# Narrow experts with two groups of 64 columns, large and small experts in turns, and weight slots of 512 columns

## The reference, cut to what matters

```
logits = xf @ router_w + router_b            # 1024 tokens x 32 experts
top_val, top_idx = top_k(logits, 4); gates = softmax(top_val)
for each expert e, with the rows xb of the tokens that chose it:
    gate, up = split(xb @ w_gu[e] + b_gu[e]) # w_gu[e]: 1024 x 2048
    gate = min(gate, 7); up = clip(up, -7, 7)
    y = ((up + 1) * gate * sigmoid(1.702 * gate)) @ w_down[e] + b_down[e]
    h[token] += gate_of_token * y            # w_down[e]: 1024 x 1024
```

## Time and profile before

| | us |
|---|---|
| median of 3 runs | 2329.13 |
| the profiled execution | 2327.12 |
| its span, first to last instruction | 2325.5 |
| TensorE busy (matmul) in it | 2261.4 |
| VectorE, ScalarE, GpSimd busy | 751.5, 374.1, 587.9 |

### The profile page before, as it was taken

The page is one execution under the profiler, slowest core; times in us unless marked ns, Lnnn a source line. Parts: engine busy times, 40 slices in busy tenths (PEclk is TensorE's granted clock), DMA queues, the critical chain, the costliest instruction groups (busy, mean ns, idle before and its releaser), DMA issues.

```text
span 2325.5 us, 36694 instructions
## 1 busy us (share of the span) xinstructions
PE 2261.4 (97%) x14520; PEld 1898.0 (82%) x14521; DVE 751.5 (32%) x1759; ACT 374.1 (16%) x845; POOL 587.9 (25%) x808
## 2 busy tenths in 40 slices
PE   8999998999987999999999999999999999999997
PEld 5664447768757999999999999998878878878876
DVE  2134776545541162222222222222222222222224
ACT  2222553323320001001111111110000000000002
POOL 1132222232232122222222222322222222222222
PEclk9999999999998999999999999999999999999999
DMA  7000213011119666777788888899999999999996
GB/s 260 1 1 19 29 35 142 28 46 37 56 37 305 220 215 217 227 228 244 254 262 270 278 270 283 283 296 317 332 323 338 321 326 337 324 328 336 324 327 229
DMA packets 377669, 506.07 MB, mean 218 GB/s; under 512 B 14887, under 2 KB 290795, under 8 KB 377448
## 3 DMA queue, kind: packets, MB, share of 16 engines
q1 hardware_dynamic: 362632, 459.56, 59.3%
q0 software_dynamic: 14864, 44.14, 7.2%
HBM read 472.17 MB, written 34.14 MB: 218 GB/s over the span
## 4 chain that ended last, share of the span: by engine, by line
PE 69%; DMA 0%; DVE 0%; issue 0%; POOL 0%; POOLq 0%; DVEq 0%
PE ps L1757 44%; PE ps L1784 12%; PE ps L1769 10%; PE ps L1736 2%; PE ps L1745 1%; DMA arena<-h_dram,arena 0%; DVE arena L1902 0%; DVE arena L2009 0%; POOL out L1636 0%; DVE arena L2015 0%; DVE arena L1995 0%; POOL small L226 0%; DVE small L223 0%; DVEq L2012 0%; POOLq L1636 0%
## 5 line engine op out<-in xcount | busy, mean ns | idle before, releaser
L1757 PEld LDWEIGHTS ps<-arena 128*128 128x128 f32 x8192 | 1029.6, 190 | 8.8 <-issue 7.7
L1757 PE MATMUL ps<-arena 128*128 128x128 f32 (+15 forms) x8192 | 1035.8, 288 | 0.8 <-DVE arena L1902 0.8
L1926 DVE TENSOR_SCALAR arena<-ps,arena 128x128 f32<-128x128 f32 (+15 forms) x256 | 94.6, 370 | 1109.9 <-PE ps L1757 1109.1
L1596 POOL TENSOR_TENSOR arena<-arena 128x128 f32<-128x128 f32 (+15 forms) x256 | 132.0, 516 | 878.0 <-DVEq L1933 878.0
L1668 ACT ACTIVATE arena<-arena 128x128 f32<-128x128 f32 (+15 forms) x256 | 83.3, 325 | 1212.5 <-DVE arena L1926 1212.5
L1784 PE MATMUL ps<-arena 128*128 128x224 f32 (+14 forms) x1920 | 272.4, 303 | 0.0
L1784 PEld LDWEIGHTS ps<-arena 128*128 128x128 f32 x1920 | 270.1, 189 | 0.2
L1769 PE MATMUL ps<-arena 128*128 128x512 f32 x544 | 236.3, 592 | 0.0
L1769 PEld LDWEIGHTS ps<-arena 128*128 128x128 f32 x544 | 102.0, 190 | 122.0 <-issue 121.7
L530 PE MATMUL ps<-arena 128*128 128x384 f32 (+1 forms) x512 | 171.7, 494 | 2.1 <-DVE arena L633 2.1
L530 PEld LDWEIGHTS ps<-arena 128*128 128x128 f32 x512 | 97.5, 193 | 68.3 <-issue 2.7
(11 more groups left out here) (274 smaller groups left out, 1617.2 us busy)
## 6 DMA issues: line engine op xcount, KB each, us to landing
arena<-in_exp_w_gu SPq DMA_DIRECT2D x256, 1024.0 KB, 7.7
arena<-in_exp_w_down SPq DMA_DIRECT2D x64, 2048.0 KB, 9.2
arena<-in_exp_b_down SPq DMA_DIRECT2D x17, 512.0 KB, 10.8
arena<-in_x SPq DMA_DIRECT2D x16, 512.0 KB, 9.0
arena<-in_w_in SPq DMA_DIRECT2D x8, 1024.0 KB, 9.6
h_dram<-arena SPq DMA_DIRECT2D x16, 512.0 KB, 2.7
arena<-in_w_out SPq DMA_DIRECT2D x1, 4096.0 KB, 13.9
arena<-h_dram SPq DMA_DIRECT2D x8, 512.0 KB, 6.9
```

The lines of the kernel that those rows point to most:

```text
L1596: v.tensor_tensor(gmn[m % 2][:, 0:n], gmn[m % 2][:, 0:n], umn[m % 2][:, 0:n], ALU.mult).then_inc(S("gum", m % 2), 1)
L1757: last = t_.matmul(bank(m % 4)[:, q * CAP:q * CAP + n], wslot[g][:, k, 256 * q + c:256 * q + c + P], xT[:, k, 0:n], start=(k == 0), stop=( ...
L1926: v.tensor_scalar(gmn[r][:, 0:n], bank(m % 4)[:, 0:n], of[:, m:m + 1], LIMIT, ALU.add, ALU.min).then_inc(S("gmn", r), 1)
```

## The change

There are four parts.

1. The widths of ranks 15 to 31 go from 128 to 128, 126, 124, 122, 120, 118, 118, 116, 114, 110, 108, 108, 106, 104, 102, 98, 88. Where an expert's width is at most 128, each matmul of `gate_up` becomes two: one for the first 64 of its 128 weight columns, with output partitions 0 to 63, and one for the other 64, with partitions 64 to 127. Both read the same N columns of `xT`.
2. The experts run in the order of ranks 0, 31, 1, 30, ..., 14, 17, 15, 16 (`ORDER`), so that a wide and a narrow one take turns up to rank 17; the table of experts is made in that order.
3. Slots 0 to 3 hold 512 columns of gate (slots 0 and 2) or of up (1 and 3), loaded as two halves of the channels, in rows of 2 KB. Slots 0 and 1 are needed for blocks 0 to 3 and freed together after block 3, slots 2 and 3 after block 7. SyncE waits for the gather after slot 1 instead of slot 0. The last expert of the order keeps the slots of before (`quarters`).
4. The loads of the wide experts are written out instead of a loop; the places that count narrow or wide experts count them along the order (`narrow_to`, `wide_to`).

The core of the diff:

```diff
-WIDTHS = (224, 204, 196, 184, 176, 168, 164, 160, 156, 152, 148, 144, 140, 136, 132) + (128,) * 17
-TILES = tuple(-(-w // P) for w in WIDTHS)
+WIDTHS = (224, 204, 196, 184, 176, 168, 164, 160, 156, 152, 148, 144, 140, 136, 132,
+          128, 126, 124, 122, 120, 118, 118, 116, 114, 110, 108, 108, 106, 104, 102, 98, 88)
+ORDER = sum(((r, NE - 1 - r) for r in range(15)), ()) + (15, 16)
+ROWS = tuple(WIDTHS[r] for r in ORDER)
+TILES = tuple(-(-w // P) for w in ROWS)
...
-            v.tensor_scalar(by_rank, iota_e[0:NE, :], own, part, ALU.is_equal, ALU.mult).then_inc(S("order"), 1)
+            v.tensor_scalar(by_rank, rank_at[0:NE, :], own, part, ALU.is_equal, ALU.mult).then_inc(S("order"), 1)
...
-            def weights(e, b):
+            def weights(e, b, quarters=False):
                 for g in range(4):
                     sp.wait_ge(S("w_used", g), b + 1)
                     for q in range(2):
-                        sp.dma_start(wslot[g][:, :, 256 * q:256 * (q + 1)],
-                                     gu_v[ds(e, 1), :, :, q, 256 * g:256 * (g + 1)].rearrange("o p k n -> (o p) k n")
-                                     ).then_inc(S(f"w_in{q}", g), 16)
-                    if g == 0:
+                        if quarters:
+                            to, of = wslot[g][:, :, 256 * q:256 * (q + 1)], gu_v[ds(e, 1), :, :, q, 256 * g:256 * (g + 1)]
+                        else:
+                            to = wslot[g][:, KH * q:KH * (q + 1), :]
+                            of = gu_v[ds(e, 1), :, KH * q:KH * (q + 1), g % 2, 512 * (g // 2):512 * (g // 2 + 1)]
+                        sp.dma_start(to, of.rearrange("o p k n -> (o p) k n")).then_inc(S(f"w_in{q}", g), 16)
+                    if g == 1:
                         for j in range(2):
                             sp.wait_ge(S("xin", j), 16)
...
-            def gate_up(b, n, between):
+            def gate_up(b, n, between, quarters=False):
 
                 for m in range(8):
-                    g, c = m // 2, (m % 2) * P
                     pe.wait_ge(S("gu_bank", m % 4), 2 * b + m // 4 + 1)
                     for q in range(2):
-                        if m % 2 == 0:
-                            pe.wait_ge(S(f"w_in{q}", g), 16 * b + 16)
+                        if quarters:
+                            g, c = m // 2, 256 * q + (m % 2) * P
+                            if m % 2 == 0:
+                                pe.wait_ge(S(f"w_in{q}", g), 16 * b + 16)
+                        else:
+                            g, c = 2 * (m // 4) + q, (m % 4) * P
                         for k in range(KT):
-                            last = t_.matmul(bank(m % 4)[:, q * CAP:q * CAP + n], wslot[g][:, k, 256 * q + c:256 * q + c + P],
-                                             xT[:, k, 0:n], start=(k == 0), stop=(k == KT - 1))
+                            if not quarters and m % 4 == 0 and k % KH == 0:
+                                pe.wait_ge(S(f"w_in{k // KH}", g), 16 * b + 16)
+                            for c0, c1 in (((0, P),) if n > P else ((0, P // 2), (P // 2, P))):
+                                last = t_.matmul(bank(m % 4)[c0:c1, q * CAP:q * CAP + n],
+                                                 wslot[g][:, k, c + c0:c + c1],
+                                                 xT[:, k, 0:n], start=(k == 0), stop=(k == KT - 1))
                     last.then_inc(S("gu_ps", m % 4), 1)
                     between(m)
...
-            def clamps(b, n, of, between):
+            def clamps(b, n, of, between, quarters=False):
...
-                    if m % 2 == 1:
+                    if quarters and m % 2 == 1:
                         dve.sem_inc(S("w_used", m // 2), 1)
+                    if not quarters and m % 4 == 3:
+                        for q in range(2):
+                            dve.sem_inc(S("w_used", 2 * (m // 4) + q), 1)
```

More of the change, by code:

```diff
@@ L27 @@
 CAP = 256
-WIDTHS = (224, 204, 196, 184, 176, 168, 164, 160, 156, 152, 148, 144, 140, 136, 132) + (128,) * 17
-TILES = tuple(-(-w // P) for w in WIDTHS)
+WIDTHS = (224, 204, 196, 184, 176, 168, 164, 160, 156, 152, 148, 144, 140, 136, 132,
[3 more added lines that the diff above has]
+TILES = tuple(-(-w // P) for w in ROWS)
 WIDE = sum(n == 2 for n in TILES)
-assert len(WIDTHS) == NE and max(WIDTHS) <= CAP and all(n == 2 for n in TILES[:WIDE])
+assert len(WIDTHS) == NE and max(WIDTHS) <= CAP and sorted(ORDER) == list(range(NE))
 NMORE = SEQ * TOPK // CAP + NE
@@ L45 @@
 C_WIDTH = C_IOTA + NE
-C_BLK = C_WIDTH + NE
+C_RANK = C_WIDTH + NE
+C_BLK = C_RANK + NE
 C_HALF, C_EPS = C_BLK + NMORE, C_BLK + NMORE + 1
@@ L1482, in program @@
         LAST = NE - 1
-        assert TILES[LAST] == 1 and LAST > WIDE
+        assert TILES[0] == 2 and TILES[LAST - 1] == TILES[LAST] == 1
         def more_expert(eng, i):
@@ L1496, in wide_to, with narrow_to @@
         def wide_to(r):
-            return min(r, WIDE)
+            return sum(n == 2 for n in TILES[:r])
+        def narrow_to(r):
+            return r - wide_to(r)
         ffn = ExitStack()
@@ L1519, in weights @@
                                  ).then_inc(S("w_in0", g), 16)
[L1521 to L1524, removed]
+            for r in range(NE):
                 e = main_expert(sp, r)
[L1526 to L1530, removed]
+                weights(e, r, quarters=r == LAST)
+                if TILES[r] == 1:
+                    q = narrow_to(r)
+                    if q >= 2:
+                        sp.wait_ge(S("bd_used"), q - 1)
+                    sp.dma_start(bd_row[q % 2], exp_b_down[0, ds(e, 1), :].rearrange("o n -> (o n)").partition_broadcast(P)
+                                 ).then_inc(S("bd_in", q % 2), 16)
             def load_h(t):
@@ L1951, in rows_out_main @@
                     return
-                if r >= 0 and m == 3:
+                if m == 3:
                     if r:
@@ L1955, in rows_out_main @@
                     rows_out(0, tiles_to(r), rec[r % 3])
-                if r >= 0 and m == 4:
-                    if TILES[r] == 2:
-                        rows_out(1, tiles_to(r), rec[r % 3])
+                if m == 4:
+                    rows_out(1, tiles_to(r), rec[r % 3])
                     dve.drain()
@@ L1982, in _ @@
                     rows_out_narrow(r - 1)
-                clamps(r, WIDTHS[r], eb[r % 2], (lambda m: rows_out_main(r - 1, m)) if r < LAST else tiles_between)
+                clamps(r, ROWS[r], eb[r % 2], (lambda m: rows_out_main(r - 1, m)) if r < LAST else tiles_between,
+                       quarters=r == LAST)
                 if r + 1 < NE:
@@ L2002, in _ @@
             dve.wait_ge(S("hg_in"), 16)
-            dve.wait_ge(S("bd_in", LAST % 2), 16 * ((LAST - WIDE) // 2 + 1))
-            v.scalar_tensor_tensor(hg, bd_row[LAST % 2], gate, hg, ALU.mult, ALU.add)
+            b_last = narrow_to(LAST)
+            dve.wait_ge(S("bd_in", b_last % 2), 16 * (b_last // 2 + 1))
+            v.scalar_tensor_tensor(hg, bd_row[b_last % 2], gate, hg, ALU.mult, ALU.add)
             dve.drain()
@@ L2058, in _constants @@
     c[:, C_WIDTH:C_WIDTH + NE] = np.array(WIDTHS)
+    c[:, C_RANK:C_RANK + NE] = np.array(ORDER)
     c[:, C_BLK:C_BLK + NMORE] = np.arange(NMORE)
```

40 lines of the change are left out of this document (22 added, 18 removed).

## The result

The changed kernel takes 2306.81 us (median, 2305.74 to 2310.14) against 2329.86 for the kernel before beside it (2328.21 to 2331.12): a ratio of 0.990, with a 95% interval of 0.9887 to 0.9921. It is faster, by 23 us, where 49 were forecast, and lies 4 us above the range. The profiled execution has a span of 2304.1 us.

What follows compares the result with a forecast made beforehand. TensorE, busy for 97% of the span, was taken to bound the kernel. Pace gain less issue, edges, order and start, 67.7 - 3.6 - 14.1 - 0.5 - 0.5 = 49.0 us, gave a median of 2280 us, range 2270 to 2303.

Steps and rivals of the forecast that it cites:

- Pace, N / 1.2 + 2.5: Narrow experts' gate-and-up: a pair of 64-column matmuls takes N / 1.2 plus 2.5 ns; gain 67.7 us.
- Second rival: Narrow gate-and-up: the two column groups overlap less; 2518 us with loads added, 2695 without overlap; chance 0.03.
- Issue: Narrow gate-and-up at 88 to 104 moving columns: TensorE's sequencer needs 87 ns a pair; cost 3.6 us.
- first rival: All narrow gate-and-up pairs: TensorE's sequencer is the bound at 62 ns a matmul; 2398 us; chance 0.07.
- Edges, 47 x 0.30 = 14.1 us: Narrow gate-and-up: each way between 64-column and 128-column work and back costs 0.30 us, 47 times.
- Order: Wide experts' down matmuls follow only 8 transposes and may wait for hT; 0.5 us for all 15, ends 0 and 2.
- Just enough cover: Down matmuls of width 132: work before k = 7 just hides the 2.1 us hT chain; larger widths have more.
- Slots, 0: Weight slots of 512 columns: 2 KB runs load at 390 GB/s, over 14 us of slack each; cost nothing.
- the start, 0.5: First expert: two slots load ahead of the gather and block 0 wants both; cost 0.5 us, ends 0 and 3.
- third rival: Last wide-and-narrow pairs: weight transfers bind; 2290 us; chance 0.05.
- the prediction's sign of late weights: TensorE idle at a gate-and-up's 1st or 5th block would show the weight slots forecast wrong; no size given.
- Fourth rival: Routing: an expert's token count exceeds its width and opens a further block of 256 columns; 2380 to 2400 us; chance 0.03.

Runs made afterwards that it cites:

- the first experiment: The changed kernel, but with scatters of 128 rows for every narrow expert whatever its width: 2279.21 us, ratio 0.9780.

## Why the prediction was wrong, step by step

- **What bounds the kernel: right.** TensorE's time is the kernel's time; with the scatters mended the kernel takes 2279.2 us, and the sum said 2280. That it comes so close is partly luck: issue was put 2.3 us too high and the order 1.5 too low.
- **The missing term: the step that failed.** Nowhere does the prediction cost the scatters. The change alters their row counts with the widths (part 1), and the sum put that at nothing without a reason. Scatters of 118, 118 and 122 rows landed after 28 to 30 us, stopped GpSimd and through it TensorE, and cost about 25 of the 27.6 us that scatters of 128 rows gave back. It could have been seen before: among the second tiles in the trace of before those of 96, 76 and 68 rows land in 7.9, 12.0 and 11.5 us, the smaller ones later. And the earlier trace rows measured the `hT` chain of an undisturbed block, without the two waits that lie ahead of it on GpSimd.
- **Pace, N / 1.2 + 2.5: right.** The narrow `gate_up` of the first experiment, less 1.75 us of transposes and 0.8 of edges, gives pairs of 84.1 (98 rows), 90.7 (106), 94.0 (110) and about 109 ns (128): N / 1.2 + 2.4. At that pace the 17 experts take 417.9 us, forecast 418.3. Second rival, loads added: not seen.
- **Issue: price right, place wrong, 3.6 us forecast, 1.3 measured** (two pauses in the expert of 88 rows alone: 0.56 and 0.22 us idle, but 0.8 and 0.4 by the starts). The 44 ns of the earlier trace rows is near the floor that the kernel of 64 rows shows (48 to 51), but it holds for blocks of 128 matmuls with their transposes in between, not for each pair. The first rival, 62 ns for each matmul by the Trainium skill (TensorE: Matmul & The Clock Gate), is refuted for this program: 29.5 ns each in bursts, and 38 in the expert of 88 rows.
- **Edges, 47 x 0.30 = 14.1 us: right**, by the timeline (0.31) and by 18 edges taken away.
- **Order, 0.5 us forecast, about 2.0 measured**: the starts at the 14th and 15th record of a wide expert's down matmuls come late, by nothing at widths 196 to 224, by 0.03 to 0.28 us in sum at the others and by 0.31 at 148. Less the 0.18 us that the kernel before loses at 132, they are 2.0 us. "Just enough cover" misread: from 1561.30 to the next group's start, 1575.88 in the trace of before, it is 14.58 us where 128 starts of 112.5 ns give 14.40, so the expert of width 132 waited 0.18 us already. The prediction's upper end was 2. The front text's wait of SyncE for the gather is against a constant and holds only at the first expert.
- **Slots, 0, and the start, 0.5: right for the steady part**, as the kernel with quarters everywhere shows; the third rival did not come in this order. TensorE did stand behind the 5th block, which looks like the prediction's sign of late weights, but it waited for VectorE, and the pauses went with the scatters. At the start the difference is the clock, which was not in the sum and doesn't belong to the change.
- **Fourth rival, a count above its width:** no, no further block was run.
- **The range** reached 23 us above the forecast for known costs and had no room for an operation that wasn't in the list.

## What to carry to other kernels

When a size changes, go through every instruction whose shape has that size in it, the DMAs first: for an indirect DMA over partitions, like this scatter, ask for the largest divisor up to 16, not for the bytes. A transfer that is off the critical path is safe only as long as what waits for its landing has nothing urgent queued behind it on the same engine. And a step that is cheap for one shape should be read at all shapes that the trace already has, as a slow second tile was there to be seen.

## What the runs showed of the hardware beyond that

- An indirect accumulating DMA of 127 rows of 4 KB takes 53.2 us, of 126 rows 8.4, of 128 rows 9.0.
- Two groups of 64 columns hide their loads fully: a pair takes N / 1.2 + 2.4 ns where a load of 128 columns takes 111.4 at N = 88; at N = 64 a pair takes 59 ns between pauses.
- TensorE's instructions come in blocks of 128 matmuls with their loads; with the DMA share at 1.0 a block mostly takes 6.1 to 6.6 us, and the wait appears as "issue" with no releaser, 1.3 to 1.6 us behind a packet of the "instruction" queue.
- After 16.6 us of standing still, TensorE's clock of 1.2 GHz lasted into the first matmuls of the expert part, none in some executions and up to 13 (8.6 us instead of 6.2 for 32 of them) in others: differences of 2 us at the start say nothing about a change.
